# Projecting the ML stage's two output-gate units behind the key sums of the neighbourhood attention

## What is computed

```python
pl = jnp.split(modulate(xl, g_mix[l], sh1, sc1) @ w_in[l], IN_OFFSETS, axis=-1)
qa_l, ka_l, va_l = na_project(pl, na_qk_gain[l])
oa_l = neighbourhood_attention(qa_l, ka_l, va_l, ka_c, va_c, na_rpb[l])
...
hb_l, _, _ = mlstm_bidir(qb_l, kb_l, vb_l, gb_l, st_f, st_b)
ob_l = mlstm_output(hb_l, pl[6], ml_head_gain[l])

def mlstm_output(h, o, head_gain):
    B, H, T, d = h.shape
    hn = rms_norm(h.transpose(0, 2, 1, 3), head_gain)
    out = hn * jax.nn.sigmoid(o.reshape(B, T, H, d).astype(jnp.float32))
    return out.reshape(B, T, H * d).astype(o.dtype)
```

## Time and profile before

| | us |
|---|---|
| median of 3 runs | 2172.21 (2169.93 to 2174.93) |
| the profiled execution's own time | 2174.71 |
| its span in the trace | 2172.9 |
| mean granted TensorE clock | 0.969 |
| TensorE busy | 2046.5 (94%) |
| VectorE / ScalarE / GpSimd busy | 1139.5 / 757.2 / 645.1 |

### The profile page before, as it was taken

One profiled execution on the slowest core, in us unless ns is written; L12 is line 12 of the kernel. 1 busy time (PEld: TensorE's weight loads), 2 busy tenths in 40 slices (PEclk: granted clock), 3 DMA queues, 4 the chain that ended last, 5 costly groups with the idle time before them and its releaser, 6 DMA issues.

```text
span 2172.9 us, 29749 instructions
## 1 busy us (share of the span) xinstructions
PE 2046.5 (94%) x11694; PEld 1689.9 (78%) x11694; DVE 1139.5 (52%) x1975; ACT 757.2 (35%) x1209; POOL 645.1 (30%) x820
## 2 busy tenths in 40 slices
PE   7889999999989999999999998889989989999999
PEld 5777888766668888888888877688866667888887
DVE  5455433578866666277537564654368864212111
ACT  4443232546653211111111244433366643222222
POOL 1111221210002433343333431122220014555555
PEclk8999999999999999999999999997999999999999
DMA  7302431100002333233223210111110002333323
GB/s 295 114 20 72 154 97 40 48 30 10 10 11 68 112 121 100 75 129 133 88 97 117 97 59 30 32 49 40 49 49 10 10 21 78 97 97 97 99 95 107
DMA packets 76528, 166.24 MB, mean 77 GB/s; under 512 B 5224, under 2 KB 46824, under 8 KB 75376
## 3 DMA queue, kind: packets, MB, share of 16 engines
q1 hardware_dynamic: 75728, 163.18, 22.5%
q10 hardware_dynamic: 672, 1.25, 0.2%
HBM read 162.31 MB, written 2.10 MB: 76 GB/s over the span
## 4 chain that ended last, share of the span: by engine, by line
PE 81%; DVE 7%; ACT 4%; issue 4%; DMA 1%; PEld 1%; POOL 1%; SPq 0%; PEldq 0%; DVEq 0%; ACTq 0%; POOLq 0%
PE psum L1156 23%; PE psum L1157 22%; PE psum L1158 22%; PE psum L1415 1%; DMA wm<-w_mod 1%; PE psum L1769 1%; PE psum L1207 1%; ACT nap L771 1%; PE psum L1799 1%; PE psum L1406 1%; POOL wlo L584 1%; PE psum L1538 1%; PE psum L1475 1%; PE psum L1524 1%; PE psum L1476 1%
## 5 line engine op out<-in xcount | busy, mean ns | idle before, releaser
L584 POOL TENSOR_TENSOR wlo<-raw,whi 128x256 fp32r<-128x256 f32 x816 | 644.9, 822 | 1519.8 <-ACT whi L609 1519.8
L1156 PE MATMUL psum<-hhi,whi 128*128 128x512 f32 (+1 forms) x1704 | 611.5, 359 | 15.5 <-DVEq L1970 8.3
L1157 PE MATMUL psum<-hlo,whi 128*128 128x512 f32 (+1 forms) x1704 | 601.3, 353 | 0.0
L1158 PE MATMUL psum<-hhi,wlo 128*128 128x512 f32 (+1 forms) x1704 | 600.7, 353 | 0.0
L609 ACT ACTIVATE whi<-raw 128x1024 fp32r<-128x1024 f32 x204 | 215.6, 1058 | 870.9 <-PE psum L1158 864.2
L1156 PEld LDWEIGHTS psum<-hhi,whi 128*128 128x128 f32 x1704 | 325.5, 191 | 69.9 <-issue 13.5
L1158 PEld LDWEIGHTS psum<-hhi,wlo 128*128 128x128 f32 x1704 | 324.7, 191 | 44.5
L1157 PEld LDWEIGHTS psum<-hlo,whi 128*128 128x128 f32 x1704 | 325.5, 191 | 42.0 <-issue 0.5
L2621 DVE TENSOR_TENSOR ffuf<-ffsa,psum 128x768 f32<-128x768 f32 (+1 forms) x44 | 36.1, 821 | 312.7 <-ACT ffsa L1106 306.0
L2606 DVE SCALAR_TENSOR_TENSOR ffmacc<-wm,csil,ffmacc 128x256 f32<-128x256 f32 x336 | 188.6, 602 | 10.0 <-DVE ffmacc L2606 4.9
L1156 PE MATMUL psum<-uhi,whi 128*128 128x512 f32 (+1 forms) x528 | 188.4, 357 | 3.7 <-DVE ulo L2625 2.1
(11 more groups left out here) (323 smaller groups left out, 3064.5 us busy)
## 6 DMA issues: line engine op xcount, KB each, us to landing
raw<-w_stream SPq DMA_DIRECT2D x204, 512.0 KB, 3.5
wm<-w_mod SPq DMA_DIRECT2D x80, 512.0 KB, 4.0
wm<-w_mod SPq DMA_DIRECT2D x8, 1024.0 KB, 13.1
xres<-x_t SPq DMA_DIRECT2D x8, 384.0 KB, 7.2
out<-xres SPq DMA_DIRECT2D x8, 256.0 KB, 2.7
namask<-c_f ACTq DMA_DIRECT2D x2, 384.0 KB, 3.7
consts<-c_f SPq DMA_DIRECT2D x1, 254.0 KB, 2.8
narpb<-rpb ACTq DMA_DIRECT2D x2, 120.0 KB
```

The source lines that it names most:

```text
L584: nc.gpsimd.tensor_tensor(wlo[:, q % 2, c:c + UW // 4], raw[:, q % RAW, c:c + UW // 4], whi[:, q % 2, c:c + UW // 4], ALU.subtract).then_i ...
L1156: mm(dst, ah, bh, start=first, stop=False)
L1157: mm(dst, ah, bl, start=False, stop=False)
L1158: return mm(dst, al, bh, start=False, stop=last)
```

## The change

The two output-gate units move from the ML stage to the end of the two key projections of the NA stage, one for each head pair, in both layers, in place of the 40 dummy products. So the unit numbers change: `ML_O` is (4, 7), `NA_QK` is (2, 5), `NA_OUT` 8, `ML_G` 10, `ML_QK` 11; from ML_V (13) on nothing changes. ScalarE copies the gate's projection out of PSUM into a new buffer, which lies where `osig` will be, and the sigmoid later works there in place. The five units at the start of the ML stage become three. The two modulation chunks that stood behind the gate units are made elsewhere: one behind the first state updates, one at the head of the fourth head unit. SP then interleaves six raw units with ring halves, not eight.

```diff
-NA_V, NA_QK, NA_OUT = 0, 2, 6
-ML_G, ML_QK, ML_O, ML_V, ML_QK1 = 8, 9, 11, 13, 15
+NA_V, NA_QK, NA_OUT = 0, (2, 5), 8
+ML_G, ML_QK, ML_O, ML_V, ML_QK1 = 10, 11, (4, 7), 13, 15
...
-        MOD_ML = MOD_GATE + 8
+        MOD_ML = MOD_GATE + 6
...
+            def gate_out(l, pr, full):
+
+                q0 = 0 if full else CTX_LEN
+                act.wait_ge(w_used, u0(l, ML_O[pr]) + 1)
+                A(NA["oraw"][:, pr, q0:], psum_pair(psum, 0)[:, q0:], ACT.Copy)
...
                 for i in range(2):
-                    u = u0(l, ML_O) + i
-                    act.wait_ge(w_used, u + 1)
-                    A(ML["osig"][:, i, q0:], psum_pair(psum, i)[:, q0:], ACT.Sigmoid).then_inc(ml_a, 1)
-                    his(u + 3)
-                    mod_rows(MOD_GATE + 4 + i)
+                    A(ML["osig"][:, i, q0:], NA["oraw"][:, i, q0:], ACT.Sigmoid).then_inc(ml_a, 1)
                 exp_ln_table()
...
                 weights(0)
+                mod_rows(MOD_GATE + 7)
                 for i in range(MLU):
+                    if i == 3:
+                        mod_rows(MOD_GATE + 10)
                     if i < MLU - 1:
                         weights(i + 1)
...
-                    barrier(u0(l, NA_QK) + 2 * pr + 2)
+                    gate_out(l, pr, full)
+                    barrier(u0(l, ML_O[pr]) + 1)
                     att_act(l, pr)
...
-                keep_warm(40)
+                gate_out(l, 0, full)
+
+            def gate_out(l, pr, full):
+
+                u = u0(l, ML_O[pr])
+                unit(u)
+                pe.wait_ge(rs2, NAQK(l, pr, "q"))
+                feature_unit(u, 0, ranges(full))
...
                 na_sums(l, pr, "kc", 1, NA["ks"][:, 0, :], [(0, CTX_LEN)])
-                keep_warm(40)
+                gate_out(l, pr, full)
...
-                for i, pair in enumerate((0, 1, 3, 0, 1)):
+                for i, pair in enumerate((0, 1, 3)):
                     u = u0(l, ML_G) + i
                     unit(u)
-                    if i >= 3:
-                        pe.wait_ge(ml_d, D_(l, ("gates", "cv0")[i - 3]))
-                    feature_unit(u, pair, ranges(full or i < 3))
+                    feature_unit(u, pair, ranges(True))
                     mods_one()
...
                 updates(0, (bank(1), bank(4)))
+                mods_one()
 
                 for i in range(MLU):
+                    if i == 3:
+                        mods_one()
                     if i < MLU - 1:
                         exponents(i + 1)
...
-                    if i < 4:
+                    if i < 5:
                         mods_one()
                     if i == 4:
-                        mods_one()
                         latent_piece(0, (CTX_LEN, TOK))
```

More of the change, by code:

```diff
@@ L140, in na_scope @@
         def na_scope(a):
-            a("na_spare", [P, 2, TOK])
-            d = dict(qhi=a("naqhi", [P, TOK], fp32r), qlo=a("naqlo", [P, TOK], fp32r),
+            d = dict(oraw=a("na_osig", [P, 2, TOK]), qhi=a("naqhi", [P, TOK], fp32r), qlo=a("naqlo", [P, TOK], fp32r),
                      khi=a("nakhi", [P, TOK], fp32r), klo=a("naklo", [P, TOK], fp32r),
@@ L162, in ml_scope @@
         def ml_scope(a):
-            d = dict(qk1=a("mlqk1", [P, 2, TOK]), osig=a("mlosig", [P, 2, TOK]),
+            d = dict(osig=a("mlosig", [P, 2, TOK]), qk1=a("mlqk1", [P, 2, TOK]),
                      va=a("mlva", [P, TT, ML_HEADS, 65]), kt=a("mlkt", [P, TT, 256]),
@@ L692, in norm_phase @@
                     if which == 0 and k == 6:
-                        his(u0(l, NA_QK) + 1)
+                        his(u0(l, NA_QK[0]) + 1)
             def na_inputs(l, full):
-                u, q0 = u0(l, NA_QK), 0 if full else CTX_LEN
+                u, q0 = u0(l, NA_QK[0]), 0 if full else CTX_LEN
                 act.wait_ge(w_used, u0(l, NA_V) + 2)
@@ L738, in na_pair @@
             def na_pair(l, pr, full):
-                u, q0 = u0(l, NA_QK) + 2 * pr, 0 if full else CTX_LEN
+                u, q0 = u0(l, NA_QK[pr]), 0 if full else CTX_LEN
                 act.wait_ge(w_used, u + 1)
@@ L835, in ml_act @@
                 v_of(0)
-                mod_rows(MOD_GATE + 6)
+                mod_rows(MOD_GATE + 4)
                 v_of(1)
-                mod_rows(MOD_GATE + 7)
+                mod_rows(MOD_GATE + 5)
                 act.wait_ge(ml_d, D_(l, "rows"))
@@ L847, in ml_act @@
                 ins.then_inc(ml_a, 1)
-                mod_rows(MOD_GATE + 8)
+                mod_rows(MOD_GATE + 6)
                 v_of(2)
@@ L886, in ml_act @@
                 weights(0)
+                mod_rows(MOD_GATE + 7)
                 for i in range(MLU):
+                    if i == 3:
+                        mod_rows(MOD_GATE + 10)
                     if i < MLU - 1:
                         weights(i + 1)
-                    if 1 <= i <= 4:
-                        mod_rows(MOD_ML + i)
+                    if 1 <= i <= 2:
+                        mod_rows(MOD_GATE + 7 + i)
+                    if 3 <= i <= 4:
+                        mod_rows(MOD_GATE + 8 + i)
                     if i in (2, 4, 6):
@@ L1343, in na_inputs @@
                 pe.wait_ge(small_in, SMALLS["na", l])
-                u = u0(l, NA_QK)
+                u = u0(l, NA_QK[0])
                 for g in range(16):
@@ L1376, in na_inputs @@
                     pe.wait_ge(mod_add, 3)
-                keep_warm(40)
+                gate_out(l, 0, full)
[4 more added lines that the diff above has]
+                feature_unit(u, 0, ranges(full))
             def na_pair(l, pr, full):
-                u = u0(l, NA_QK) + 2 * pr
+                u = u0(l, NA_QK[pr])
                 unit(u)
@@ L2711, in weight_units @@
         for pr in range(2):
-            put(NA_QK + 2 * pr, tile(P * pr))
-            put(NA_QK + 2 * pr + 1, tile(na + P * pr))
+            put(NA_QK[pr], tile(P * pr))
+            put(NA_QK[pr] + 1, tile(na + P * pr))
             put((ML_QK, ML_QK1)[pr], tile(o_ml + P * pr))
             put((ML_QK, ML_QK1)[pr] + 1, tile(o_ml + ml + P * pr))
-            put(ML_O + pr, tile(o_ml + 3 * ml + P * pr))
+            put(ML_O[pr], tile(o_ml + 3 * ml + P * pr))
         g = np.zeros((P, KT, P), np.float32)
```

## The result

Over 20 runs each, the changed kernel takes 2174.14 us (2168.58 to 2178.92) and the kernel before 2168.18 us (2164.01 to 2175.95). The ratio is 1.0024 with a 95% interval of 1.0015 to 1.0034: about 5.2 us slower (the two medians are 6.0 apart). The forecast was 2170.9, 1.3 us faster than the three-run median of 2172.21. The time lies inside the range, but the sign is wrong, and the likeliest case (no difference that can be measured) is not what came. That the absolute time is only 3.2 us off is in part luck: the three-run median that it starts from lies 4.0 us above the median of 20.

What follows compares the result with a forecast made beforehand. TensorE, with 81% of the chain, was taken to bound the kernel. Front 33.4 won, less attention 15.0, chunks 5.9 and 4.2, clock 7, left 1.3 us won: 2170.9 us from the median 2172.21, range 2162.5 to 2176.5.

Steps and rivals of the forecast that it cites:

- Attention side: Before the four attentions: gate units, copy and extra rounding replace the dummies and delay the scores, 15.0 us lost.
- Front: Start of the ML stage: first values start earlier, 20.3 us in layer 0 and 13.1 in layer 1, 33.4 won.
- First moved chunk: Behind layer 0's state updates: ring halves issued behind raw unit 19 land late, 5.9 us lost, 4.4 of it waiting.
- Second moved chunk: Head of layer 0's fourth head unit: its second half loads late, 4.2 us lost, 2.7 of it idle.
- The clock: Layer 0's fourth and fifth head units: the new stop brings the granted clock to 1.2 GHz earlier, 7 us lost.
- The base: Whole kernel: the sum, made on a profiled 2174.71 us, is applied to the median of 2172.21, giving 2170.9.
- The first: Fourth head unit: the clock doesn't fall or comes back at once, all 8.3 us stay won, 2163.9; chance 0.32.
- The second: Chunk ring: loads in time, both chunks cost their bare 1.5 us, no stop, 15.4 us won, 2156.8; chance 0.05.
- The third: Attentions: idleness around the gate units lowers the clock, each 3 us longer, 12 us lost, 2182.9; chance 0.09.
- The fourth: ML front: something held hidden, scans or table loads, is late by 10 us, giving 2180.9; chance 0.04.

Runs made afterwards that it cites:

- the run with one rounding fewer: Changed kernel with ScalarE's rounding of one more weight unit moved from the barrier before each attention to the one behind it: 2167.67 us, ratio 1.0003.
- the run with the chunk positions alone: Kernel before with only the change's two chunk positions; gate units, dummies and SP's order stay as before: 2181.23 us, ratio 1.0061.
- The ring edit: Changed kernel with raw weight unit 19 loaded behind all chunk halves instead of ahead of the first moved chunk's two: 2165.3 us, ratio 0.9992.
- the run with both edits: Changed kernel with raw unit 19 behind all chunk halves and the second moved chunk at the fifth head unit's end: 2157.48 us, ratio 0.9947.
- the third profile: Kernel before, unaltered, profiled a third time: 2164.35 us.
- the run with dummies: Changed kernel with 20 dummy products between the turn and the second moved chunk at the fourth head unit's head: 2169.92 us, ratio 1.0010.
- three pairs of runs: Pairs differing by the second chunk's place alone, in the changed kernel, with the ring edit, and in the kernel before: 7.6, 9.8, 11.9 us.

## Why the prediction was wrong, point by point

- **Attention side, 15.0 lost: right.** 14.3 in the trace. Copy and extra rounding stand before the scores as described, and the run with one rounding fewer confirms the rounding's price.
- **Front, 33.4 won: right in the trace.** 20.4 and 13.1. The scans were hidden, and GpSimd's low half took 2.77 and 2.78 us. It ran beside VectorE's convolution, as the forecast said: in layer 0 from 236.09 to 238.86, with the first scan starting at 238.32. The lock on the shared port that the Trainium skill, page SBUF — State Buffer, describes for VectorE operations with two SBUF inputs was hardly put to the test, and nothing was lengthened. Of the 20.4 us, 1.6 come from taking the two chunks away and 18.9 from the gate units, by the run with the chunk positions alone. In the medians the gate units' move is worth 13 to 15 us where the traces give 17.7; both intervals reach that, and whether something is really missing stays open.
- **First moved chunk, 5.9: right as a number, 5.67, partly by luck.** The wait was 2.56 and not 4.4; turn and both halves at the low clock made it up. The ring edit won 7 us in the medians, give or take 4, where its term leaves 4.4; its trace has 2.7 for the stop and 3.2 for a clock that the run with both edits didn't keep.
- **Second moved chunk, 4.2: right as a number, 4.1** from 319.0 to 323.07, and luck again. 2.7 us of idleness were forecast; the stops are 0.50 for ScalarE's row, which was to end unseen, and 0.46 for the ring, and the low clock makes up the rest. That the low clock had already begun ahead of it was not in the term.
- **The clock, 7 lost: the first step that failed, by its size.** With the chunk's 4.1 taken off, exponents 2 to 8 grew by 5.7 − 4.1 + 6.5 + 2.0 = 10.1 us against the profiled execution. I had 7, because I let the clock come back before the stretch's end; it came back only after 353, inside the projection. The low stretch also began at 316.8, ahead of the first stop of the fourth unit, and not at it: the forecast's cause, the stop, isn't what the trace shows. By itself this error of 3.1 us did not turn the sign in the pair of profiles, which is 3.4 us in favour of the change where the sum had 1.3.
- **The base: the step that turned the sign.** "The profiled execution took 2174.71, 2.5 us above the median; applied to the median the sum gives 2170.9" treats the difference as an offset that both kernels share. It is not one. The profiled execution of before lies 6.5 us above the median of 20, that of the changed kernel 2.8 us below its own: −3.4 + 6.5 + 2.8 is the 6.0 us between the medians. In the traces, the execution of before had low stretches at 281 to 288 and at 334 to 343 that the third profile doesn't have (78.1 against 85.6 us), and only five of 68 timed executions have a clock as low. The changed kernel has its low stretch in both executions traced: all six traces with a second chunk at the head of the fourth unit (the changed kernel twice, the ring edit, the chunk positions alone, the rounding edit, the dummies) have 0.50 for some 30 us there; of the eight without, one has. Its twenty timed executions have a clock of 0.962 to 0.968, each below the lowest of before. So the sum credited the change with a base that was already paying part of the price. The base is off by 9.3 us in all (6.5 + 2.8), and the traces place only a part of it, since no execution of before with a time near its median was traced.
- **Rivals.** The first (the clock stays up) was given 0.32; neither trace of the changed kernel has it, nor any of the four variants that keep the chunk there. The second was not what the change did, but two edits to it bring 11.5 of its 15.4 us. The third has a mechanism that exists, at a price of about 1 us for each attention for a stop almost three times as long, and shows nothing in the changed kernel. The fourth didn't happen.
- **Shown as announced:** scores 1.9 us behind the gate unit; values 4.3 us (layer 0) and 4.2 us (layer 1) behind the key unit; a landing as releaser at the ring waits; 0.50 to the fifth unit's projection. Not as announced: the ring waits are 2.56 and 0.46 us where 4.5 and 1.4 were named.

What stays open is what brings the clock down in the fourth unit. The Trainium skill, page TensorE: Matmul & The Clock Gate, section on how the gate bites in real kernels, puts the falls of its example down to waits for DMA between short stretches of work. Here a trace without such a wait, 28.00 of 28 us busy, fell too. That the second chunk's place makes the fall far more frequent is shown by the traces, six of six against one of eight, and fits three pairs of runs (7.6, 9.8 and 11.9 us for that place, where the stops themselves are 1 to 3 us). Whether it does so by its stops or by its small products is open: the run with dummies, which was to part the two, fell in its trace and may not have fallen in half of its executions.

## What to carry to other kernels

Before a sum is made against one profiled execution, ask whether that execution has stretches at a low clock in the very stages that the change touches: an offset between profile and median may be such a stretch, and a change that makes the stretch permanent is then charged only for the difference. When work is moved out of a long projection to fill a better place, look at what travels with it: here the gate units were worth moving, and the two small chunks cost more than they weigh, since one came in behind a late item of the queue and the other at a place where the low clock then stood in every trace. Each was mended by one line of order (ring ahead of the raw unit, the chunk one unit later), and with a rounding moved behind the attention the idea is worth 0.7%.

## What the runs showed of the hardware

- One program, three executions, 2174.7, 2175.5 and 2164.4 us: behind the state updates the granted clock was 0.50 in two and 1.00 in the third at the same instructions, with TensorE busy throughout (7.00 of 7 us in the first, 8.00 of 8 in the third). From exponents 1 to exponents 2 it takes 5.5 us or 3.8.
- The clock can be at 0.50 for 28 us in which the trace shows TensorE busy without a gap.
- Idleness of 5.1 us in place of 40 dummies, four times, didn't move the scores and cost 0.21% of the kernel (0.03 to 0.39%).
- A ring half that SP issued behind a raw unit waiting for its buffer made TensorE stop for 2.56, 3.70 and 3.51 us in three executions; with the raw unit behind it there was no stop.
- A chunk of 1.5 us that stood ahead of a wait for GpSimd was nearly free: without it the wait grew from 3.39 to 4.73 us.
